# Expert gate and up weights in slabs of four rows of one matrix, and column groups of 256 columns

## The chip, the core and the metric

The kernel runs on one core of a Trainium2 chip. The metric is the device time of one execution in microseconds (us). A core has TensorE (PE; its weight loads are listed as PEld), VectorE (DVE), ScalarE (ACT), GpSimd (POOL) and SyncE (SP), which here issues the large loads. Everything is in float32; the profile shows a float32 product as two matmuls and two weight loads, and counts in it are of these.

## The reference

The input is 256 latent tokens and 256 context tokens of width 1024. Two layers of a first block (attention, Fourier mixing, and a mixture of experts) are followed by two layers of a second block with linear projections and attention. The change lies in the mixture of experts:

```
def expert_choice_ffn(h, w_router, w_gate_e, w_up_e, w_down_e):
    B, N, _ = h.shape
    cap = CAPACITY_FACTOR * N // N_EXPERTS
    aff = jax.nn.softmax((h @ w_router).astype(jnp.float32), axis=-1)
    top_aff, top_idx = lax.top_k(aff.transpose(0, 2, 1), cap)
    bidx = jnp.arange(B)[:, None, None]
    xg = h[bidx, top_idx]
    a = jnp.einsum("becd,edf->becf", xg, w_gate_e)
    u = jnp.einsum("becd,edf->becf", xg, w_up_e)
    out = jnp.einsum("becf,efd->becd", jax.nn.silu(a) * u, w_down_e) * top_aff[..., None].astype(h.dtype)
    return jnp.zeros_like(h).at[bidx, top_idx].add(out)
```

There are 16 experts, each takes 32 tokens of a token set, and gate, up and down are 1024 x 1024 each: 12 MiB of weights an expert and layer. Layer 0 has two token sets (latent and context), layer 1 one.

## The kernel before

**The ring.** All large weights pass through `ring`, four slots of 2 MiB, in the order of `slab_plan` (L52). SyncE (L597 to L603) waits until the slot's old slab is released (`slab_used`, counted by TensorE's `last_release`, L715), and issues the DMAs of the next slab as `loads` (L302) lists them. TensorE waits for a slab in `slab_wait`.

**An expert** has six slabs. Slabs 0 to 3 each hold 256 rows of the gate matrix and the same 256 rows of the up matrix, two rows for each partition (two DMAs of 1 MiB, 8 KB in a row for each partition). Slabs 4 and 5 hold 512 rows each of the down matrix, four rows for each partition (one DMA of 2 MiB, 16 KB in a row). The plan weaves in some slabs of the memory projection (xkv) in experts 6 to 13 of layer 1. A few slabs of expert 1 are loaded ahead of time by GpSimd into free buffers (`EARLY`, `load_early`, L617).

**The gate and up product** (L1142 to L1166) works with four column groups of TensorE, 32 columns wide each: the gathered tokens of an expert (`XGT`, 128 x 32) are the stationary operand, and the weights in the ring are the moving operand. Groups 0 and 1 take 512 columns each of gate, groups 2 and 3 of up, and each writes all 512 columns of its own 32 partitions of bank `ps[s]`, one bank for each token set `s`. A slab gives two row steps `k`, so 16 recorded matmuls of 512 columns for a token set.

**Behind it** ACT copies the bank into `GU` (L1760). TensorE turns it with four transposes (L1181), whose stationary operand is `GU` at every fourth column, so that channel 4p + c comes to partition p, as the down matrix has its rows. ACT makes the sigmoid of the gate part (L1771), DVE multiplies it by gate (L2378) and by up (L2383) into `HE`. The down product (L1194) is made by four column groups of 256 columns each. DVE scales and places its rows (L2395). From the fifth expert on each expert also scatters rows of an earlier group of four (L1125), and in the first twelve the rows for the next group of four are gathered (L1024, then ACT at L1705).

**Rows by pairs.** Since a slab has rows 2p and 2p + 1 in partition p, the 1024 channels of the tokens are dealt out in the same manner, by `paired` (L289): in the transposes of the normed tokens (L981), in the gathers (L1024), in the columns of the ada product for the second norm (L697), in the router table and in three vectors (`PAIRED`, L248, turned at L679 and copied at L2053).

Of the kernel before, what the change touches and what calls it, by code (L numbers as in the profile page):

```python
# [19 lines left out]
ALU = mybir.AluOpType  # L20
# [3 lines left out]
P = 128  # L24
D = 1024
# [138 lines left out]
def build(nc, a, out, ctx):  # L164
# [136 lines left out]

    def loads(kind, l, s):  # L302
# [310 lines left out]
    def _(gp):  # L613
        def load(dst, src, name):
            gp.dma_start(dst, src).then_inc(sem(name), 16)

        def load_early(l, q):  # L617

            for half, name in zip(EARLY_AT[l, q], ("w_gate_e", "w_up_e")):
                load(half.rearrange("p (k n) -> p k n", k=2),  # L620
                     a[name][l, 1, 2 * P * q:2 * P * (q + 1), :].rearrange("(p k) n -> p k n", p=P), f"early{l}{q}")
# [10 lines left out]
        for l in range(DEPTH):  # L632
# [8 lines left out]
            load(WR[:, l].rearrange("p (q i) e -> p q i e", i=2), a["w_router"][l].rearrange("(q p i) e -> p q i e", p=P, i=2), "ld_const")  # L641
# [29 lines left out]
    def _(pe):  # L671
# [285 lines left out]
        def experts(l):  # L957
# [1814 lines left out]
```

## Time and profile before

| what | value |
|---|---|
| runs, median (lowest to highest) | 2285.1 us (2284.4 to 2285.84), 3 runs |
| the profiled execution | 2280.98 us, its span 2279.1 us |
| TensorE busy, share of the span | 1986.8 us, 87% |
| VectorE, ScalarE busy | 623.2 us, 435.3 us |
| bytes moved by DMA, mean rate | 576.03 MB, 253 GB/s |
| granted TensorE clock, mean | 0.969 |

The profile is of one execution. Its span is the time from the first to the last instruction in it; the execution's own time has a little more around it. A busy time is the union of an engine's instructions. "Idle before" is the time in which an engine stood still ahead of an instruction, with the one that released it behind the arrow. A granted clock of 1.00 is 2.4 GHz, and one of 0.50 would be 1.2 GHz; values between are means over a stretch.

### The profile page before, as it was taken

To read this page: it belongs to the slowest core of one execution; us is meant where nothing else is said; L and a number is where in the kernel's file an instruction comes from. 1 tells how busy PE (TensorE), PEld (TensorE's weight loads), DVE (VectorE), ACT (ScalarE), POOL (GpSimd) and SP (SyncE) were. 2 spreads that over 40 slices of the span, in tenths; PEclk is the share of its full clock that TensorE was granted. 3 is DMA by queue.
4 is the path that set the end of the run, shared out by engine and by line. 5 is a ranking of instruction groups with operands and counts; after the bars stand their busy time and mean duration, and the time that the engine had idled before them with its cause. 6 is when DMAs were issued, how large, how long until landed. Compare 5 with 4: busy or idle time off the path is not lost.

```text
span 2279.1 us, 31723 instructions
## 1 busy us (share of the span) xinstructions
PE 1986.8 (87%) x13681; PEld 1093.5 (48%) x13681; DVE 623.2 (27%) x1483; ACT 435.3 (19%) x1095; POOL 26.9 (1%) x52
## 2 busy tenths in 40 slices
PE   7999999999988898889999975667776699999997
PEld 4445554456434444334768641233432347564765
DVE  2012640135112221223351321201101235333533
ACT  2122621013111111002161110100000122222222
POOL 3000000000000000000000000000000000000000
PEclk9999999999999999999999997889989999999999
DMA  9544244227899999994314589999999933233320
GB/s 290 185 160 173 75 142 171 94 74 272 349 424 421 423 422 422 420 419 170 129 57 185 217 353 424 423 416 415 418 415 419 364 111 111 87 135 111 111 83 19
DMA packets 133832, 576.03 MB, mean 253 GB/s; under 512 B 7448, under 2 KB 16128, under 8 KB 92736
## 3 DMA queue, kind: packets, MB, share of 16 engines
q1 hardware_dynamic: 129312, 556.82, 61.8%
q0 software_dynamic: 3872, 17.00, 2.2%
q8 instruction: 110, 1.80, 0.3%
q10 hardware_dynamic: 512, 0.19, 0.0%
q14 instruction: 26, 0.21, 0.0%
HBM read 572.93 MB, written 1.05 MB: 252 GB/s over the span
## 4 chain that ended last, share of the span: by engine, by line
PE 53%; DMA 19%; issue 10%; PEld 8%; DVE 5%; PEldq 2%; ACT 2%; SPq 0%; POOL 0%; DVEq 0%; POOLq 0%
DMA ring<-w_up_e 14%; PE ps L788 8%; PE ps L1159 6%; PE ps L1250 5%; PE ps L973 4%; PE ps L1258 3%; PEld ps L1194 3%; PE ps L804 2%; PE ps L1392 2%; PE ps L777 2%; PEldq L717 2%; DMA ring<-w_xkv 2%; DMA ring<-w_down_e 2%; PE ps L1226 1%; PE ps L1229 1%
## 5 line engine op out<-in xcount | busy, mean ns | idle before, releaser
L1159 PE MATMUL ps<-ring,reg_bc 128*32 128x512 f32 x2960 | 382.4, 653 | 125.9 <-DMA ring<-w_up_e 118.1
L1159 PEld LDWEIGHTS ps<-ring,reg_bc 128*32 128x32 f32 x2960 | 91.9, 115 | 393.7 <-DMA ring<-w_up_e 199.8
L788 PE MATMUL ps<-reg_a,ring 128*128 128x512 f32 (+1 forms) x768 | 253.9, 488 | 5.5 <-issue 4.4
L788 PEld LDWEIGHTS ps<-reg_a,ring 128*128 128x128 f32 x768 | 143.5, 190 | 104.6 <-issue 92.7
L2352 DVE TENSOR_TENSOR xall<-xall,ps 128x512 f32<-128x512 f32 x48 | 32.8, 687 | 446.0 <-PE ps L1125 446.0
L1250 PE MATMUL ps<-ring,reg_a 128*128 128x512 f32 (+2 forms) x448 | 142.7, 474 | 2.6 <-issue 2.3
L1760 ACT ACTIVATE reg_bc<-ps 128x512 f32<-128x512 f32 x48 | 28.7, 597 | 562.4 <-PE ps L1159 562.4
L2395 DVE TENSOR_TENSOR reg_a<-ps,reg_e 32x256 f32<-32x256 f32 x192 | 80.7, 420 | 199.8 <-PE ps L1194 197.4
L1194 PE MATMUL ps<-ring,reg_bc 128*32 128x256 f32 x2048 | 117.8, 380 | 16.2 <-issue 14.7
L777 PE MATMUL ps<-ring,reg_a 128*128 128x512 f32 (+1 forms) x288 | 112.8, 546 | 1.9 <-issue 1.5
L1250 PEld LDWEIGHTS ps<-ring,reg_a 128*128 128x128 f32 x448 | 74.0, 190 | 65.1 <-issue 63.7
L1194 PEld LDWEIGHTS ps<-ring,reg_bc 128*32 128x32 f32 x2048 | 70.3, 110 | 54.7 <-issue 21.1
L1194 PE MATMUL ps<-ring,reg_e 128*32 128x256 f32 x1024 | 67.2, 406 | 31.4 <-issue 17.6
L1258 PE MATMUL ps<-reg_a,ring 128*128 128x256 f32 x384 | 88.9, 390 | 6.1 <-ACT reg_d L1798 5.0
L804 PE MATMUL ps<-reg_d,ring 128*128 128x512 f32 (+1 forms) x256 | 84.2, 488 | 1.7 <-issue 0.8
L973 PE MATMUL ps<-ring,reg_bc 128*128 128x512 f32 x192 | 84.2, 594 | 0.6 <-issue 0.5
L1258 PEld LDWEIGHTS ps<-reg_a,ring 128*128 128x128 f32 x384 | 74.0, 196 | 17.0 <-issue 7.0
L777 PEld LDWEIGHTS ps<-ring,reg_a 128*128 128x128 f32 x288 | 54.2, 190 | 56.2 <-issue 54.5
L804 PEld LDWEIGHTS ps<-reg_d,ring 128*128 128x128 f32 x256 | 48.1, 190 | 35.6 <-issue 30.4
L1568 ACT ACTIVATE reg_e<-ps 128x512 f32<-128x512 f32 (+1 forms) x48 | 23.6, 491 | 207.9 <-PE ps L788 207.8
L1194 PEld LDWEIGHTS ps<-ring,reg_e 128*32 128x32 f32 x1024 | 34.5, 116 | 57.1 <-issue 29.2
L1705 ACT ACTIVATE reg_bc<-ps,modt,scl 128x128 f32<-128x128 f32 x96 | 36.2, 458 | 129.2 <-PE ps L1024 129.2
(356 smaller groups left out, 2161.5 us busy)
## 6 DMA issues: line engine op xcount, KB each, us to landing
ring<-w_down_e SPq DMA_DIRECT2D x64, 2048.0 KB, 14.9
ring<-w_gate_e SPq DMA_DIRECT2D x123, 1024.0 KB, 10.6
ring<-w_up_e SPq DMA_DIRECT2D x123, 1024.0 KB, 13.6
ring<-w_in SPq DMA_DIRECT2D x34, 2048.0 KB, 8.1
ring<-w_ada SPq DMA_DIRECT2D x24, 2048.0 KB, 8.2
ring<-w_out SPq DMA_DIRECT2D x8, 2048.0 KB, 7.9
ring<-w_xkv SPq DMA_DIRECT2D x8, 1024.0 KB, 14.1
ring<-w_br_global SPq DMA_DIRECT2D x4, 1024.0 KB, 6.4
```

The source lines that it names most:

```text
L717: pe.drain().then_inc(slab_used, 1)
L777: mm = pe.matmul(ps[t][:, c0:COL], HT[:, k, t * P:t * P + P], w[:, k, c0:COL], start=(k == 0), stop=(k == KC - 1))
L788: mm = pe.matmul(ps[j][:, 0:n], w[:, k, j * P:(j + 1) * P], HT[:, k, 0:n], start=(k == 0), stop=(k == KC - 1))
L804: mm = pe.matmul(ps[n % 4][:, 0:tokens], w[:, k, j * P:(j + 1) * P], OT[:, k, 0:tokens], start=(k == k0), stop=(k == k1 - 1))
L973: mm = pe.matmul(ps[b][:, :], MT[:, k, t * P:t * P + P], w[:, k, :], start=(k == 0), stop=(k == KC - 1))
L1159: mm = pe.matmul(ps[s][32 * j:32 * j + 32, :], XGT[l][:, e // 4, s, 2 * q + k, e % 4 * CAP:(e % 4 + 1) * CAP], w[j // 2][:, k, (j % 2) * C ...
L1194: mm = pe.matmul(ps[4 + s][32 * j:32 * j + 32, 0:SEQ], HE[l][:, s, k, q * CAP:(q + 1) * CAP], w[:, k, j * SEQ:(j + 1) * SEQ], start=(q == ...
L1250: fill(name, lambda b: [pe.matmul(ps[b][:, 0:c1 - c0], src[:, k, t * P:t * P + P], w[:, k, c0:c1], start=(k == 0), stop=(k == KC - 1)) for ...
L1258: fill(name, lambda b: [pe.matmul(ps[b][:, 0:SEQ], w[:, k, c * P:(c + 1) * P], src[:, k, :], start=(k == 0), stop=(k == KC - 1)) for k in ...
L1392: yield pe.matmul(ps[b][:, :], OT2[:, k, t * P:t * P + P], w[:, k, :], start=(q == 0), stop=(q == KC - 1))
L1705: ins = act.activation(XGT[l][:, g, s, k, :], ps[6 + h][:, kk * P:(kk + 1) * P], ACT.Identity, scale=SCL[:, l, 1, k, s:s + 1], bias=MODT[: ...
L2395: ins = dve.tensor_tensor(OE[l][r:r + CAP, e // 4 % 2, s, j * SEQ:(j + 1) * SEQ], ps[4 + s][CAP * j:CAP * (j + 1), 0:SEQ], GB[CAP * j:CAP ...
```

## The change

**Slabs.** Slab 0 and 1 of an expert now hold 512 rows of gate each, slab 2 and 3 the same of up, four rows for each partition, by one DMA of 2 MiB. The early slabs keep two DMAs of 1 MiB, each with two of the four rows.

**Column groups.** Each of the four groups takes 256 columns of the one matrix. Group j takes those of the half j // 2 whose number modulo 4 is 2 (j mod 2) or one more, so the moving operand is read at a stride of four floats, and the output stands in one piece of 256 columns, gate in the left half of the bank and up in the right. A slab gives four row steps, so 32 recorded matmuls of 256 columns for a token set.

**Behind it.** The transposes read adjacent columns of `GU`. Their outputs, the sigmoid and the two products are pieces of 256 columns, and the down product picks its stationary columns from `HE` accordingly.

**Rows by fours.** `paired` and what follows it go by four rows instead of two. The wait for the second half of the gathered rows stands ahead of slab 1 instead of slab 2.

```diff
@@ GU, EG, RG, HE, PAIRED
-        EG.append(reg_bc[:, eg:eg + ns * SEQ].rearrange("p (s c n) -> p s c n", s=ns, c=4))
+        EG.append(reg_bc[:, eg:eg + ns * SEQ].rearrange("p (s n) -> p s n", s=ns))
...
-    PAIRED = reg_e[0:24, 0:2 * P]
+    PAIRED = reg_e[0:12, 0:4 * P]
@@ paired, loads
-        return slice(k // 2 * 2 * P + k % 2, (k // 2 + 1) * 2 * P, 2)
+        return slice(k // 4 * 4 * P + k % 4, (k // 4 + 1) * 4 * P, 4)
...
+    def gate_or_up(l, e, part):
+
+        rows4 = a[("w_gate_e", "w_up_e")[part // 2]][l, e, 4 * P * (part % 2):4 * P * (part % 2 + 1), :]
+        return rows4.rearrange("(p k) n -> p k n", p=P)
...
-                return [(c0, 2, D, a[name][l, e, 2 * P * part:2 * P * (part + 1), :].rearrange("(p k) n -> p k n", p=P))
-                        for c0, name in ((0, "w_gate_e"), (2 * D, "w_up_e"))]
+                return [(0, 4, D, gate_or_up(l, e, part))]
@@ load_early
-            for half, name in zip(EARLY_AT[l, q], ("w_gate_e", "w_up_e")):
-                load(half.rearrange("p (k n) -> p k n", k=2),
-                     a[name][l, 1, 2 * P * q:2 * P * (q + 1), :].rearrange("(p k) n -> p k n", p=P), f"early{l}{q}")
+            for n, half in enumerate(EARLY_AT[l, q]):
+                load(half.rearrange("p (k n) -> p k n", k=2), gate_or_up(l, 1, q)[:, 2 * n:2 * n + 2, :], f"early{l}{q}")
@@ turn_biases
-            for i in range(2):
-                pe.transpose(ps[0][:, P + 24 * i:P + 24 * (i + 1)], PAIRED[:, i:2 * P:2], ident[0:24, 0:24])
+            for i in range(4):
+                pe.transpose(ps[0][:, P + 12 * i:P + 12 * (i + 1)], PAIRED[:, i:4 * P:4], ident[0:12, 0:12])
@@ the experts on TensorE
-                    w = [half.rearrange("p (k n) -> p k n", k=2) for half in gate_up]
-                    if q % 2 == 0 and e % 4 == 0:
-                        pe.wait_ge(*at(f"xgt@{l}", (e // 4 + 1) * 2 * ns - 1 + q // 2))
+                        pairs2 = slot(i)[:, 0:2 * D], slot(i)[:, 2 * D:4 * D]
+                    w = [two.rearrange("p (k q i r) -> p k q r i", k=2, q=2, r=4) for two in pairs2]
+                    up, half = q // 2, q % 2
+                    if q < 2 and e % 4 == 0:
+                        pe.wait_ge(*at(f"xgt@{l}", (e // 4 + 1) * 2 * ns - 1 + q))
...
-                        for k in range(2):
+                        for k in range(4):
                             for j in range(4):
-                                mm = pe.matmul(ps[s][32 * j:32 * j + 32, :],
-                                               XGT[l][:, e // 4, s, 2 * q + k, e % 4 * CAP:(e % 4 + 1) * CAP],
-                                               w[j // 2][:, k, (j % 2) * COL:(j % 2 + 1) * COL],
-                                               start=(q == 0 and k == 0), stop=(q == 3 and k == 1))
+                                mm = pe.matmul(ps[s][32 * j:32 * j + 32, up * SEQ:(up + 1) * SEQ
+                                                     ].rearrange("p (r i) -> p r i", r=2),
+                                               XGT[l][:, e // 4, s, 4 * half + k, e % 4 * CAP:(e % 4 + 1) * CAP],
+                                               w[k // 2][:, k % 2, j // 2, 2 * (j % 2):2 * (j % 2) + 2, :],
+                                               start=(half == 0 and k == 0), stop=(half == 1 and k == 3))
...
-                        mm = pe.transpose(ps[2 + s][:, c * P:(c + 1) * P], GU[l][:, s, c:COL:4], ident[:, :])
+                        mm = pe.transpose(ps[2 + s][:, c * P:(c + 1) * P], GU[l][:, s, c * P:(c + 1) * P], ident[:, :])
...
-                                               HE[l][:, s, k, q * CAP:(q + 1) * CAP],
+                                               HE[l][:, s, k % 2 * P + (2 * q + k // 2) * CAP:k % 2 * P + (2 * q + k // 2 + 1) * CAP],
@@ the sigmoid on ACT, the products on DVE
-                    gate = ps[2 + s][:, :].rearrange("p (c n) -> p c n", c=4)[:, :, 0:2 * CAP]
-                    act.activation(EG[l][:, s], gate, ACT.Sigmoid).then_inc(sem(f"eg@{l}"), 1)
+                    act.activation(EG[l][:, s], ps[2 + s][:, 0:SEQ], ACT.Sigmoid).then_inc(sem(f"eg@{l}"), 1)
...
-                    dve.tensor_tensor(HE[l][:, s], RG[l][:, s], turned[:, :, 2 * CAP:4 * CAP], ALU.mult
+                    dve.tensor_tensor(HE[l][:, s], RG[l][:, s], ps[2 + s][:, SEQ:COL], ALU.mult
```

The lines below are the order of instructions on one engine. `ps` is PSUM, `ring` the weight ring, `reg_bc` holds `XGT`, `GU` and `HE` of layer 0, `tmp` the selection matrices and `reg_d` the normed tokens; here the counts are of products as the engine gets them in the program, grouped, with one row for a run of equal instructions. TensorE, one middle expert of layer 0 and the start of the next, before:

```order
L1159 MATMUL ps<-ring,reg_bc 32x512 x64
L1125 MATMUL ps<-reg_a,reg_e 128x512 x2
L1181 MATMUL ps<-ident,reg_bc 128x128 x8
L1194 MATMUL ps<-ring,reg_bc 32x256 x32
L1024 MATMUL ps<-tmp,reg_d 128x128 x8
L1194 MATMUL ps<-ring,reg_bc 32x256 x32
L1035 MATMUL ps<-ident,reg_e 128x128 x2
```

And the same place now:

```order
L1163 MATMUL ps<-ring,reg_bc 32x256 x128
L1128 MATMUL ps<-reg_a,reg_e 128x512 x2
L1186 MATMUL ps<-ident,reg_bc 128x128 x8
L1199 MATMUL ps<-ring,reg_bc 32x256 x32
L1027 MATMUL ps<-tmp,reg_d 128x128 x8
L1199 MATMUL ps<-ring,reg_bc 32x256 x32
L1038 MATMUL ps<-ident,reg_e 128x128 x2
```

The 64 gate and up products of 512 columns have become 128 of 256; nothing else has moved. SyncE, the head of the expert slabs of layer 0 behind the last ada slabs, before:

```order
L602 DMA ring<-w_out 128x8x512 x2
L602 DMA ring<-w_ada 128x8x512 x4
L602 DMA ring<-w_gate_e 128x2048
L602 DMA ring<-w_up_e 128x2048
...
L602 DMA ring<-w_down_e 128x4096 x2
```

And now:

```order
L606 DMA ring<-w_out 128x8x512 x2
L606 DMA ring<-w_ada 128x8x512 x4
L606 DMA ring<-w_gate_e 128x4096 x2
L606 DMA ring<-w_up_e 128x4096 x2
L606 DMA ring<-w_down_e 128x4096 x2
```

Four pairs of gate and up DMAs have become two DMAs of gate and two of up, each of the shape of the down slabs.

## Rows read from the trace of the kernel before

**Rows 1.** The page: the chain that ended last by line, and a DMA issue.
```profile
DMA ring<-w_up_e 14%; PE ps L788 8%; PE ps L1159 6%; PE ps L1250 5%; PE ps L973 4%; PE ps L1258 3%; PEld ps L1194 3%; PE ps L804 2%; PE ps L1392 2%; PE ps L777 2%; PEldq L717 2%; DMA ring<-w_xkv 2%; DMA ring<-w_down_e 2%; PE ps L1226 1%; PE ps L1229 1%
...
ring<-w_gate_e SPq DMA_DIRECT2D x123, 1024.0 KB, 10.6
```

**Rows 2.** Groups by line: count, busy us, mean ns, idle before and releasers.
```profile
L1159 PE MATMUL ps<-ring,reg_bc 128*32 128x512 f32 x2960 | 382.4, 653 | 125.9 <-DMA ring<-w_up_e 118.1 <-issue 4.8
```

**Rows 3.** Windows: us, busy PE, PEld, DVE, ACT, POOL; granted clock, DMA share, GB/s.
```profile
700.00:760.00 60.00, 53.05 (x560) 23.83 (x556) 13.04 (x30) 6.31 (x16) 0.00 (x0) 1.00 1.01 423
1520.00:1580.00 60.00, 41.67 (x289) 22.03 (x282) 5.15 (x12) 3.88 (x9) 0.00 (x0) 0.91 1.02 416
```

**Rows 4.** Timeline of TensorE, layer 0: start us, us, operation, idle before and releaser.
```profile
556.13 7.38 PE L1159 MATMUL ps<-ring,reg_bc 128*32 128x512 f32 x64 [0.30 <-issue]
...
671.12 7.39 PE L1159 MATMUL ps<-ring,reg_bc 128*32 128x512 f32 x64
...
702.44 11.13 PE L1159 MATMUL ps<-ring,reg_bc 128*32 128x512 f32 x96 [0.29 <-issue]
...
714.27 3.64 PE L1159 MATMUL ps<-ring,reg_bc 128*32 128x512 f32 x32 [0.70 <-DMA ring<-w_up_e]
...
720.14 1.12 PE L1181 MATMUL ps<-ident,reg_bc 128*128 128x128 f32 x8
...
722.21 3.66 PE L1194 MATMUL ps<-ring,reg_bc 128*32 128x256 f32 x64 [0.95 <-issue]
...
732.23 7.38 PE L1159 MATMUL ps<-ring,reg_bc 128*32 128x512 f32 x64 [0.29 <-issue]
...
913.52 7.39 PE L1159 MATMUL ps<-ring,reg_bc 128*32 128x512 f32 x64
...
940.76 3.64 PE L1159 MATMUL ps<-ring,reg_bc 128*32 128x512 f32 x32 [0.27 <-issue]
...
1023.22 7.42 PE L1194 MATMUL ps<-ring,reg_bc 128*32 128x256 f32 x128 [0.94 <-issue]
```

**Rows 5.** Timeline, layer 1: the first slab, then the slabs of one expert.
```profile
1325.86 3.96 PE L1159 MATMUL ps<-ring,reg_bc 128*32 128x512 f32 x32
1325.97 1.51 ACT L1705 ACTIVATE reg_bc<-ps,modt,scl 128x128 f32<-128x128 f32 x4 [0.38 <-PE ps L1024]
...
1386.14 1.93 PE L1194 MATMUL ps<-ring,reg_e 128*32 128x256 f32 x32 [1.46 <-DMA ring<-w_down_e]
...
1391.10 3.62 PE L1159 MATMUL ps<-ring,reg_bc 128*32 128x512 f32 x16 [3.03 <-DMA ring<-w_up_e]
...
1396.09 1.93 PE L1159 MATMUL ps<-ring,reg_bc 128*32 128x512 f32 x16 [1.37 <-DMA ring<-w_up_e]
...
1406.05 1.92 PE L1159 MATMUL ps<-ring,reg_bc 128*32 128x512 f32 x16 [1.64 <-DMA ring<-w_up_e]
...
1415.84 3.22 PE L1194 MATMUL ps<-ring,reg_e 128*32 128x256 f32 x32 [1.91 <-DMA ring<-w_down_e]
```

**Rows 6.** Instructions of single lines: duration ns min/median/max, first and last start.
```profile
L1181 PEld LDWEIGHTS ps<-ident,reg_bc x192: 195/209/221, 577.1 to 1792.4; 128*128 128x128 f32 x192
...
L981 PEld LDWEIGHTS ps<-ident,reg_d x48: 194/209/231, 495.8 to 1303.3; 128*128 128x128 f32 x48
...
L743 PEld LDWEIGHTS ps<-ident,reg_d x32: 139/140/143, 1038.0 to 1058.5; 128*128 128x128 f32 x32
...
L697 PE MATMUL ps<-ring,ct x1536: 272/273/422, 13.5 to 1311.3; 128*32 128x128 f32 x192
...
L1159 PE MATMUL ps<-ring,reg_bc x2960: 589/592/1063, 556.1 to 1790.4; 128*32 128x512 f32 x198
```

**Rows 7.** Timeline of TensorE: ada products at stride two, adjacent, and adjacent transposes.
```profile
190.99 2.04 PE L697 MATMUL ps<-ring,ct 128*32 128x128 f32 x64
...
208.67 1.95 PE L697 MATMUL ps<-ring,ct 128*32 128x128 f32 x64
...
1050.12 1.04 PE L743 MATMUL ps<-ident,reg_d 128*128 128x128 f32 x8
```

More of the change, by code:

```diff
@@ L242, in build @@
         GU.append(reg_bc[:, gu:gu + ns * COL].rearrange("p (s n) -> p s n", s=ns))
-        EG.append(reg_bc[:, eg:eg + ns * SEQ].rearrange("p (s c n) -> p s c n", s=ns, c=4))
-        RG.append(reg_bc[:, rg:rg + ns * SEQ].rearrange("p (s c n) -> p s c n", s=ns, c=4))
+        EG.append(reg_bc[:, eg:eg + ns * SEQ].rearrange("p (s n) -> p s n", s=ns))
+        RG.append(reg_bc[:, rg:rg + ns * SEQ].rearrange("p (s n) -> p s n", s=ns))
         hidden = reg_e[:, 1024:1280] if he is None else reg_bc[:, he:he + ns * SEQ]
-        HE.append(hidden.rearrange("p (s c n) -> p s c n", s=ns, c=4))
+        HE.append(hidden.rearrange("p (s n) -> p s n", s=ns))
         OE.append(reg_a[:, 0:2048 * ns].rearrange("p (b s d) -> p b s d", b=2, s=ns))
-    PAIRED = reg_e[0:24, 0:2 * P]
+    PAIRED = reg_e[0:12, 0:4 * P]
     YT = reg_e[:, 4096:5120].rearrange("p (b n) -> p b n", b=2)
@@ L640, in _ @@
                      a[f"diff_lambda_{v}_2"][l:l + 1, :].broadcast_to([P, 32]), "ld_const")
-            load(WR[:, l].rearrange("p (q i) e -> p q i e", i=2), a["w_router"][l].rearrange("(q p i) e -> p q i e", p=P, i=2), "ld_const")
+            load(WR[:, l].rearrange("p (q i) e -> p q i e", i=4), a["w_router"][l].rearrange("(q p i) e -> p q i e", p=P, i=4), "ld_const")
         for t in range(2):
@@ L1145, in experts @@
                         pe.wait_ge(sem(f"early{l}{q}"), 32)
-                        gate_up = EARLY_AT[l, q]
+                        pairs2 = EARLY_AT[l, q]
                     else:
@@ L1942, in _ @@
             for n, v in enumerate((a["b_ada"][l, 3 * D:4 * D], a["b_ada"][l, 4 * D:5 * D], a["norm2_g"][l])):
-                load_vec("ld_vec0", PAIRED[12 * l + 4 * n:12 * l + 4 * n + 4, :], v.rearrange("(q c) -> q c", c=2 * P))
+                load_vec("ld_vec0", PAIRED[6 * l + 2 * n:6 * l + 2 * n + 2, :], v.rearrange("(q c) -> q c", c=4 * P))
         act.wait_ge(*at("vec1t", 1))
@@ L2049, in bias_columns @@
             link(dve.tensor_copy(vec0t[:, :], ps[0][:, 0:P]))
-            pairs_in = ps[0][:, P:P + 48].rearrange("p (i l n q) -> p l n q i", i=2, l=DEPTH, n=3)
+            pairs_in = ps[0][:, P:P + 48].rearrange("p (i l n q) -> p l n q i", i=4, l=DEPTH, n=3)
             for l in range(DEPTH):
                 for n, c in enumerate((24, 32, 56)):
-                    ins = dve.tensor_copy(vec0t[:, 64 * l + c:64 * l + c + 8].rearrange("p (q i) -> p q i", i=2),
+                    ins = dve.tensor_copy(vec0t[:, 64 * l + c:64 * l + c + 8].rearrange("p (q i) -> p q i", i=4),
                                           pairs_in[:, l, n])
@@ L2375, in experts @@
                     m = e * ns + s
-                    turned = ps[2 + s][:, :].rearrange("p (c n) -> p c n", c=4)
                     dve.wait_ge(*at(f"eg@{l}", m + 1))
-                    dve.tensor_tensor(RG[l][:, s], EG[l][:, s], turned[:, :, 0:2 * CAP], ALU.mult
+                    dve.tensor_tensor(RG[l][:, s], EG[l][:, s], ps[2 + s][:, 0:SEQ], ALU.mult
                                       ).then_inc(sem(f"rg@{l}"), 1)
```

1 line of the change is left out of this document (removed).

## Prediction

> **What bounds the kernel now.** I read the chain and the DMA issues on the page, the groups by line, the windows over the two expert stretches, and last TensorE's timeline inside one expert of each layer. The chain that ended last has the DMA of w_up_e as its first single item, 14% [rows 1]. The gate and up product, L1159, is the costliest group: 2960 recorded matmuls, 382 us busy, 118 us of idle time ended by that DMA [rows 2]. The change touches almost nothing outside the expert stretches (556 to 1031 us in layer 0, from 1326 us on in layer 1), so I took one window in each. In both the DMA engines are full, share 1.01 and 1.02, at 423 and 416 GB/s; in layer 0 TensorE is busy 53 us of 60 beside that, in layer 1 only 42 [rows 3]. So both are bound by transfers, layer 1 with room to spare, layer 0 with TensorE close behind.
>
> How close shows in the timeline of layer 0 [rows 4]. One expert starts its gate product at 702.44 us, the next at 732.23: 29.79 us, of which TensorE waited 0.70 for a DMA. Its own work is 29.1 us. From 671.12 to 913.52 experts 4 to 11 pass, 30.3 us each. The other eight gather no rows or scatter none and have less to do: expert 12 takes 27.24 us (913.52 to 940.76).
>
> **What the transfers gain.** In layer 1 TensorE waits for each slab, so its starts are the landings [rows 5]. Gate/up slabs land 4.96 us after what went before (1386.14 to 1391.10), 4.99, and the next two 9.96 together; the two down slabs behind them take 9.79 together, 4.90 each. All are 2 MiB. A gate/up slab is now two DMAs with 8 KB runs for each partition, a down slab one DMA with 16 KB runs; after the change every expert slab has exactly the second form. That is 0.07 us a slab. There are 123 gate/up slabs [rows 1]; some four at the head of each layer have landed before they are wanted, which leaves 115: 115 x 0.07 = 8 us, four in each layer. The transfers of one expert then take 6 x 4.90 = 29.4 us instead of 29.7. Whether the longer runs or the DMA fewer give it, I can't tell, and both go together. The bound below is nothing: if a down slab is quick only for what goes before it, there is no gain.
>
> The Trainium skill, "DMA: Bandwidth & Descriptors" (Anatomy of one DMA), gives each DMA a fixed 2 us beside its bytes over 436 GB/s; by that, 123 DMAs fewer would save up to 246 us. The landings speak against it: pairs of 1 MiB land every 4.98 us, so the fixed part already lies beside other transfers.
>
> **What TensorE pays.** Three edits meet on it.
>
> First, the gate/up matmuls are twice as many and half as wide. The down product has that form already: 64 matmuls of 256 columns take 3.66 us, 32 of 512 take 3.64 [rows 4]. The twice as many weight loads lie under the streaming there as well. 0.02 us a slab of layer 0, 0.1 us an expert.
>
> Second, the transposes of the hidden rows read adjacent columns and no longer every fourth. Their weight loads take 209 ns in the median, loads of adjacent columns 140 [rows 6]; eight such transposes took 1.12 us [rows 4], eight of adjacent columns 1.04 [rows 7]. That gives back 0.1 us an expert, on the path from the gate to the down product. The two cancel. Sigmoid and products read the same elements of PSUM, now in one piece: 0, between a few tens of ns either way.
>
> Third, and this decides: each matmul now reads its moving operand, the weights in the ring, at a stride of four floats. No row shows that form. The nearest is the ada product, four column groups of 128 columns: 64 matmuls take 1.95 us where columns are adjacent and 2.04 where they are every second one [rows 7], 0.09 more. If that is a price of the instruction, a slab of layer 0, now 64 matmuls, pays 0.09, an expert 0.36. If it is a pace of reading, more comes out: 2.04 less the 0.27 of one matmul [rows 6], over 15 steps of four, is 118 ns for 128 columns; the wide product takes 3.64 less 0.59 over 7 steps, 436 ns for 512 columns, 109 for 128. Nine ns for each 128 columns, 32 such a slab: 0.3 us, 1.2 an expert. The bounds are nothing, should the wide streams hide it, and twice the streaming time. Of stride four against stride two only weight loads tell: the transposes at four (L1181) and at two (L981) both load in 209 ns [rows 6]. A longer stride cost nothing there, so I stay with the nearest row, 0.36.
>
> Own work of a middle expert becomes 29.1 + 0.1 - 0.1 + 0.36 = 29.5 us, against 29.4 of transfers: level. I let layer 0 keep half of its 4 us, since the two now trade waits. Layer 1 keeps all: with one set of tokens a slab costs TensorE 1.9 us, and 3.6 at the low clock, inside 4.9 [rows 5].
>
> **Small edits.** The router table, the norm vectors, the ada columns and the turned tiles go by four instead of two. Two transposes more at the start, 0.3 us each, lie beside the first weight DMA; the gathers' weight loads go from stride two to four, no change by the two medians above. The second half of the gathered rows is wanted at slab 1 instead of slab 2: in layer 1 ACT finishes it at 1325.97 + 1.51 = 1327.48 us, and the first slab's products, begun at 1325.86 and 1.9 long, end at 1327.8 [rows 5]. So 0, and a few tenths of a us once if that cover goes. SyncE issues one DMA where it issued two; it waits for free slots, not for issue: 0. The slabs that POOL loads early stay two DMAs of 1 MiB: 0.
>
> **Sum.** -4 in layer 1, -2 in layer 0: -6 us on the profiled execution of 2281.0 us, 2275. The median of the runs lies 4.1 us higher, so I forecast 2279.
>
> **Rivals.**
> *The stride is a pace.* 1.2 us an expert: own work 30.3, above 29.4. The middle eight then take what they take now, 30.3; the first four, which find slabs landed, pay 5 us; layer 1 gives 4; some waits for DMAs stay. +4, between 0 and +12: about 2289. For it: the 118 ns. Against it: 0.09 us can as well be a gap in a row of 64 short instructions.
>
> *Every column opens a new line of SBUF (slower).* At stride four each float lies 16 bytes on, and four column groups read at once. At half pace a slab of layer 0 goes from 3.64 to 7.3 us, an expert's own work from 29.1 to 43.7. The middle eight: 8 x (43.7 - 30.3) = 107. The other eight, which now take 232 us of the 474.5 between 556.13 and the end of the last down product (1023.22 + 7.42), 29.0 each: 8 x (27.2 + 14.6 - 29.0) = 102. Less layer 1's 4: +205, 2490. It decides from some 0.3 us a slab on; at a fifth more streaming time, 0.7 us, it is 8 x 1.6 + 8 x 1.0 - 4 = +17, 2302. Against it: 209 ns at stride two and at four alike. For it: no moving operand is read so here, and never by four groups at once.
> The Trainium skill, "SBUF — State Buffer" (Door 1: The DMA port swizzle), states such a rule: lines of 16 bytes, at least two hits on a line for full speed. The weight-load rows don't agree: they pay at stride two, where two hits remain, and no more at four.
>
> *The transfers gain nothing.* Then layer 0 pays up to 2 us, layer 1 nothing: 2285 to 2287.
>
> **Chances.** Forecast 0.48, pace 0.24, new lines 0.17, no gain 0.11. A measurement of this kernel tells a change from none from about 0.2% on, 4.6 us. The forecast's own range is -11 to -3, mostly beyond that: faster 0.44. Same, 2280.5 to 2289.7: the rest of the forecast, the case without gain, half of the pace: 0.25. Slower, the other half and the new lines: 0.31. The range goes from 2274, where all of the 8 us and the shorter transposes are kept, to 2303, a fifth more streaming time, which takes in the pace; it leaves out the strong form of new lines and a little more.
>
> **What would show it.** Gate/up slabs of layer 1 landing 4.90 us apart and not 4.98: the gain is there. The 64 strided matmuls of a slab of layer 0 in 3.66 to 3.75 us: forecast; near 4.0: pace; 4.3 and more: new lines, with a DMA share in the windows of layer 0 below 1.0 and under 400 GB/s. The transposes of L1181 at 140 ns a load. The forecast is wrong if layer 0's stretch grows beyond 474.5 us, or if layer 1 doesn't shrink by at least 3.

## The result, and the profile after

| | before | after |
|---|---|---|
| median (lowest to highest) | 2284.75 us (2282.17 to 2285.84), 4 runs | 2568.66 us (2565.67 to 2570.11), 4 runs |
| ratio, with its 95% interval | | 1.1243 (1.1223 to 1.1262) |
| span of the profiled execution | 2279.1 us | 2563.7 us |
| TensorE busy | 1986.8 us, 87% | 2362.9 us, 92% |
| VectorE, ScalarE busy | 623.2, 435.3 us | 623.2, 435.4 us |
| granted TensorE clock, mean | 0.969 | 0.991 |

The change costs 284 us. The forecast was 2279 with 2303 as its upper end: it is wrong, and in its sign too. The rival of the new lines, 2490, is the one that has its side.

The page of the kernel after, the chain that ended last by engine and by line, the costliest groups (busy us, mean ns, idle before and its releaser), and the DMA issues:

```profile
PE 73%; DMA 8%; issue 8%; PEld 4%; DVE 4%; ACT 2%; PEldq 1%; SPq 0%; DVEq 0%
...
L1163 PE MATMUL ps<-ring,reg_bc 128*32 128x256 f32 x5920 | 695.0, 632 | 43.3 <-DMA ring<-w_up_e 18.8
...
L1027 PEld LDWEIGHTS ps<-tmp,reg_d 128*128 128x128 f32 x384 | 91.3, 328 | 15.6 <-issue 14.9
...
L1199 PE MATMUL ps<-ring,reg_bc 128*32 128x256 f32 x2048 | 117.1, 380 | 16.3 <-issue 14.8
...
ring<-w_up_e SPq DMA_DIRECT2D x63, 2048.0 KB, 9.8
ring<-w_gate_e SPq DMA_DIRECT2D x60, 2048.0 KB, 8.9
```

The gate and up product, L1163 now, is busy for 695.0 us where it was 382.4, and its idle time falls from 125.9 to 43.3 [rows 2]: in layer 0, as the rows below show, TensorE no longer waits for weights, the weights wait for TensorE. One of its matmuls takes 632 ns. The down product L1199 has the same form, 32 stationary columns and 256 moving ones from the same ring, and takes 380. What differs is that it reads adjacent columns.

The windows after, two in layer 0 and three in layer 1 (columns as in [rows 3]), and below them the first 60 us of layer 1 before:

```profile
720.00:780.00 60.00, 57.39 (x542) 22.89 (x538) 5.38 (x14) 3.85 (x9) 0.00 (x0) 1.00 0.75 277
840.00:900.00 60.00, 56.80 (x574) 27.70 (x578) 10.76 (x26) 5.36 (x13) 0.00 (x0) 1.00 0.73 268
...
1597.00:1657.00 60.00, 53.98 (x471) 24.73 (x474) 5.04 (x12) 6.48 (x16) 0.00 (x0) 0.97 0.77 306
1657.00:1717.00 60.00, 43.96 (x434) 14.93 (x430) 11.78 (x45) 9.21 (x16) 0.00 (x0) 0.97 1.00 421
...
1980.00:2040.00 60.00, 52.00 (x436) 25.44 (x432) 6.41 (x14) 3.50 (x8) 0.00 (x0) 1.00 1.01 424
```

```profile
1326.00:1386.00 60.00, 43.57 (x396) 17.53 (x391) 5.87 (x14) 7.43 (x18) 0.00 (x0) 0.89 0.96 400
```

In layer 0 the DMA engines have fallen from 1.01 and 423 GB/s [rows 3] to 0.75 and 277, TensorE is busy 57 of 60 us at full clock: the bound has changed. In layer 1 they are full again from the second window on, but the first moves 306 GB/s where it moved 400.

TensorE's timeline after, the head and layer 0, then layer 1 (columns as in [rows 4]):

```profile
559.23 3.92 PE L700 MATMUL ps<-ring,ct 128*32 128x128 f32 x64
...
564.40 7.73 PE L1027 MATMUL ps<-tmp,reg_d 128*128 128x128 f32 x32 [0.51 <-DVE tmp L2273]
...
576.24 7.50 PE L1163 MATMUL ps<-ring,reg_bc 128*32 128x256 f32 x64 [0.29 <-issue]
...
805.75 30.15 PE L1163 MATMUL ps<-ring,reg_bc 128*32 128x256 f32 x256 [0.29 <-issue]
...
837.98 1.04 PE L1186 MATMUL ps<-ident,reg_bc 128*128 128x128 f32 x8
...
844.06 3.97 PE L1027 MATMUL ps<-tmp,reg_d 128*128 128x128 f32 x16 [0.39 <-issue]
...
851.91 30.07 PE L1163 MATMUL ps<-ring,reg_bc 128*32 128x256 f32 x256 [0.29 <-issue]
...
1291.79 7.42 PE L1199 MATMUL ps<-ring,reg_bc 128*32 128x256 f32 x128 [0.99 <-issue]
...
1597.51 3.81 PE L1163 MATMUL ps<-ring,reg_bc 128*32 128x256 f32 x32
...
1675.97 3.81 PE L1163 MATMUL ps<-ring,reg_bc 128*32 128x256 f32 x32 [1.84 <-DMA ring<-w_gate_e]
1680.86 3.82 PE L1163 MATMUL ps<-ring,reg_bc 128*32 128x256 f32 x32 [1.08 <-DMA ring<-w_gate_e]
1685.75 3.88 PE L1163 MATMUL ps<-ring,reg_bc 128*32 128x256 f32 x32 [1.07 <-DMA ring<-w_up_e]
...
2083.26 1.93 PE L1199 MATMUL ps<-ring,reg_e 128*32 128x256 f32 x32 [0.80 <-DMA ring<-w_down_e]
```

A slab of layer 0 takes 7.50 us and not 3.64. An expert has no wait for a DMA left; the next begins 46.16 us behind it (805.75 to 851.91) where it was 30.3 [rows 4]. The 284.6 us between the two spans stand in four places:

| stretch | before | after | more |
|---|---|---|---|
| up to the first slab of layer 0 | 556.13 | 576.24 | 20.1 |
| layer 0, to the end of its last down product | 474.5 | 723.0 | 248.5 |
| from there to the first slab of layer 1 | 295.2 | 298.3 | 3.1 |
| layer 1, to the end of its last down product | 475.0 | 487.7 | 12.7 |

**Layer 0.** 64 slabs at 7.50 - 3.64 = 3.86 us more are 247. Twelve gathers of 16 matmuls take 3.97 us each; the row of one before, from its timeline in layer 0:

```profile
696.44 2.12 PE L1024 MATMUL ps<-tmp,reg_d 128*128 128x128 f32 x16 [0.36 <-issue]
```

12 x 1.85 = 22. The transposes L1186 give 16 x 0.1 back. That is 267; the stretch has grown by 248.5, so some 19 us of what is added don't show. TensorE's idle time in the stretch falls from 51.5 to 37.6 us, which is 14 of them: work now lies where TensorE waited before. The last 5 stay open.

**Layer 1.** Slabs land 4.89 us apart (1675.97, 1680.86, 1685.75), as the forecast has it, and the stretch is longer all the same. A slab costs TensorE 3.81 us and no longer 1.92, so it hands slots back later at the head, where slabs lie ready: in the first 60 us (400 - 306) GB/s x 60 us = 5.6 MB fewer arrive, which is 13.3 us of transfers at 424 GB/s. That is the whole 12.7. Behind those 60 us the mean rate to the end of the stretch is 418 GB/s in both kernels, so the faster landings bring nothing there: one window of 60 us (1897 to 1957) has only 401 GB/s, with TensorE busy for 54.8 us of it. The granted clock of the stretch is 0.88 before, where TensorE is busy 324 of 475 us, and 0.99 after, where it is busy 413 of 488.

**The head.** Eight ada products for the second norm read every fourth column now, 3.84 to 3.92 us each and not 2.04 [rows 7], and four gathers stand ahead of the first slab: 12 x 1.85 = 22, of which 20 show.

### The profile page after: what moved, and what is told of

Read it like the earlier page. It is cut to its first block, busy times and chain, and to the rows that moved or that the text cites. A ratio compares the mean times of both kernels' runs of the same rounds, so it can differ in the third digit from the quotient of the medians.

```text
span 2563.7 us, 37748 instructions
## 1 busy us (share of the span) xinstructions
PE 2362.9 (92%) x16755; PEld 1257.1 (49%) x16755; DVE 623.2 (24%) x1483; ACT 435.4 (17%) x1095; POOL 26.8 (1%) x52
## 4 chain that ended last, share of the span: by engine, by line
PE 73%; DMA 8%; issue 8%; PEld 4%; DVE 4%; ACT 2%; PEldq 1%; SPq 0%; DVEq 0%
PE ps L1163 23%; PE ps L791 8%; PE ps L1199 5%; PE ps L1255 4%; DMA ring<-w_up_e 4%; PE ps L1027 3%; PE ps L976 3%; PE ps L1263 3%; PE ps L807 2%; PE ps L1397 2%; PE ps L780 2%; PE ps L700 2%; PE ps L1128 2%; DMA ring<-w_down_e 1%; PE ps L502 1%
## 5 line engine op out<-in xcount | busy, mean ns | idle before, releaser
L1163 PE MATMUL ps<-ring,reg_bc 128*32 128x256 f32 x5920 | 695.0, 632 | 43.3 <-DMA ring<-w_up_e 18.8
L1163 PEld LDWEIGHTS ps<-ring,reg_bc 128*32 128x32 f32 x5920 | 210.4, 125 | 509.8 <-issue 450.3
L1199 PE MATMUL ps<-ring,reg_bc 128*32 128x256 f32 x2048 | 117.1, 380 | 16.3 <-issue 14.8
L1027 PE MATMUL ps<-tmp,reg_d 128*128 128x128 f32 x384 | 94.6, 404 | 6.6 <-issue 5.9
L1027 PEld LDWEIGHTS ps<-tmp,reg_d 128*128 128x128 f32 x384 | 91.3, 328 | 15.6 <-issue 14.9
L1199 PEld LDWEIGHTS ps<-ring,reg_bc 128*32 128x32 f32 x2048 | 70.1, 110 | 55.2 <-issue 21.6
L1199 PE MATMUL ps<-ring,reg_e 128*32 128x256 f32 x1024 | 63.4, 388 | 26.9 <-issue 21.9
L700 PE MATMUL ps<-ring,ct 128*32 128x128 f32 x1536 | 65.6, 331 | 3.7 <-DMA ring<-w_ada 3.7
```

The lines of the kernel that those rows point to most:

```text
L700: mm = pe.matmul(ps[b][32 * j:32 * j + 32, 0:P], CT[:, k, :], w[:, k, paired(j) if 6 <= s < 10 else slice(j * P, j * P + P)], start=(k == ...
L1027: mm = pe.matmul(ps[6 + h][:, kk * P:(kk + 1) * P], XN[:, 2 * s + t, paired(k)], SEL[:, s, t, g * P:(g + 1) * P], start=(t == 0), stop=(t ...
L1163: mm = pe.matmul(ps[s][32 * j:32 * j + 32, up * SEQ:(up + 1) * SEQ].rearrange("p (r i) -> p r i", r=2), XGT[l][:, e // 4, s, 4 * half + k, ...
L1199: mm = pe.matmul(ps[4 + s][32 * j:32 * j + 32, 0:SEQ], HE[l][:, s, k % 2 * P + (2 * q + k // 2) * CAP:k % 2 * P + (2 * q + k // 2 + 1) * CAP],
```

## The experiments

What is measured in each is the row of its first slab in layer 0: 64 matmuls of 256 columns, four column groups at once, so 16 steps of four. Kernels with one run have no interval. They differ from the kernel before by 1.8% and more, but e2 lies only 0.4% above e1 and e3 0.15% above the kernel after; what is read from these is the slab, not the time.

**One group of runs: only the stride of the moving operand.** The four kernels are the kernel after with another view of the same slab, and as many columns. The output of each matmul is one piece of 256 adjacent columns of the bank in all of them, so the writing side stays as it is.

```diff
-  w[k // 2][:, k % 2, j // 2, 2 * (j % 2):2 * (j % 2) + 2, :]   # after: every 4th column
+  w[k // 2][:, k % 2, j * SEQ:(j + 1) * SEQ]                    # e1: adjacent
+  w[k // 2][:, k % 2, j // 2, j % 2, :]                         # e2: every 2nd
+  w[k // 2][:, k % 2, 64 * j:64 * j + 768:3]                    # e5: every 3rd
+  w[k // 2][:, k % 2, 2 * j:2 * j + 2, :]                       # e3: every 8th
```

> The changed kernel, but each column group of the gate and up product reads 256 adjacent columns of the weights instead of every fourth (so the channels come out in another order, and the output differs); all else, the four-row slabs, the 256-column matmuls, the gathers and ada columns at stride four, stays. Theory (lines of 16 bytes: what costs is that each column opens a new one): the 64 matmuls of a slab of layer 0 go from 7.4-7.5 us to 3.66; what stays is 20 us ahead of layer 0, 3 ahead of layer 1, 1.9 us for each gather, less the faster landings: 2300 to 2320. Rival (the form costs: twice as many matmuls, four groups writing two places of a bank): the slab stays above 6 us and the time above 2500.

> As e1_adjacent, but every second column (8 bytes apart; output differs). If a line costs 1.77 ns and a column 0.83 ns, whichever is more, two columns on a line come to 0.885 ns a column: 16 steps of 256 columns 0.227 us apart, the slab of layer 0 about 3.9 us, the time 10 to 25 us over e1_adjacent. If only the second hit on a line matters, as the rule of two hits says, there is no difference to e1_adjacent. If any stride halves the pace: 7.4 us a slab.

> As e1_adjacent, but every third column (12 bytes apart; groups overlap, output differs). Three of four columns open a new line: 1.33 ns a column, steps 0.34 us apart, slab 5.6 us, time 2400 to 2430. If it is all or nothing at 16 bytes: 3.7 to 3.9 us a slab. If every column that has no second hit pays in full: near 5.6 as well.

> As the changed kernel, but every eighth column (32 bytes apart; output differs). A line of 16 bytes: no more than at stride four, slab 7.4 to 7.5 us, time within 10 us of the changed kernel's 2569. If the four groups contend for banks, or if lines are of 32 bytes, it is clearly slower than stride four, up to 15 us a slab.

The rows of the timeline, e1, e2, e5 and e3 in turn:

```profile
576.05 3.66 PE L1163 MATMUL ps<-ring,reg_bc 128*32 128x256 f32 x64 [0.29 <-issue]
```

```profile
579.54 3.83 PE L1163 MATMUL ps<-ring,reg_bc 128*32 128x256 f32 x64 [0.28 <-issue]
```

```profile
576.05 5.69 PE L1163 MATMUL ps<-ring,reg_bc 128*32 128x256 f32 x64 [0.29 <-issue]
```

```profile
574.32 7.57 PE L1163 MATMUL ps<-ring,reg_bc 128*32 128x256 f32 x64 [0.29 <-issue]
```

| columns | time of the kernel | slab | one matmul | step | lines of 16 bytes a step | ns a line |
|---|---|---|---|---|---|---|
| adjacent (e1) | 2314.92 us, 4 runs | 3.66 us | 379 ns | 0.219 us | 256 | 0.85 |
| every 2nd (e2) | 2323.66, 1 run | 3.83 | 388 | 0.229 | 512 | 0.448 |
| every 3rd (e5) | 2441.95, 1 run | 5.69 | 510 | 0.345 | 768 | 0.450 |
| every 4th (after) | 2568.66, 4 runs | 7.50 | 632 | 0.458 | 1024 | 0.447 |
| every 8th (e3) | 2572.47, 1 run | 7.57 | 640 | 0.462 | 1024 | 0.451 |

A step is the slab less one matmul (its median), over 15; its 1024 columns open so many lines of 16 bytes as the table says. From stride two on the step is 0.447 to 0.451 ns for each line, within 1%, and from stride four to eight it doesn't grow: what is paid is the line, not the distance. Adjacent columns are bound by something else, 0.219 us for 1024 columns, 0.214 ns each. The step is the longer of the two, 0.214 ns a column or 0.448 ns a line. The cut is not an all or nothing at stride four: stride three pays already, and two per line pay 0.17 us a slab. The times came out as expected but for two: e5 lies 12 us above its 2400 to 2430, and e2 only 9 us over e1, where 10 to 25 were expected.

The ada products of the kernel after give the same price from another instruction, four groups of 128 columns at stride four:

```profile
140.57 3.84 PE L700 MATMUL ps<-ring,ct 128*32 128x128 f32 x64
```

One of its matmuls takes 0.41 us in the median, so a step is (3.84 - 0.41) / 15 = 0.229 us for 512 columns on 512 lines: 0.447 ns a line.

e1 is also the proof of place: with the stride gone, and that alone, 254 of the 284 us go. What is left, a ratio of 1.0135 (1.0113 to 1.0157), the next experiments divide.

**Adjacent pairs (e4), and rows dealt by DVE (e6).** e4 deals out the columns otherwise: group j takes two adjacent columns of every four. The output stands in one piece as before the edit, and the transposes read `GU` by twos. e6 also has DVE write the normed rows in the order by fours, so that the turned tiles and the gathers read adjacent columns.

```diff
+  two.rearrange("p (k q i h r) -> p k q h i r", k=2, q=2, h=2, r=2)      # e4, e6: pairs 16 bytes apart
+  GU[l][:, s, c // 2 * SEQ + c % 2:(c // 2 + 1) * SEQ:2]
+  XN[:, t, :].rearrange("p (q r i) -> p q i r", q=2, r=4)                # e6: what DVE writes
+  XN[:, 2 * s + t, k * P:(k + 1) * P]                                    # e6: what a gather reads
```

> The changed kernel, the same 256 columns for each group, but read in pairs: two adjacent columns, then the next two 16 bytes on; the transposes behind it pick every second column of the bank. Two columns to a line of 16 bytes, so 0.895 ns a column: slab of layer 0 3.83 us as in e2_stride2, time 2320 to 2330. If it is the step to the next place that costs, not the lines per column: above 5.5 us a slab. If adjacent pairs cost nothing: 3.66 and 2315.

> e4_pairs, and DVE writes the normed rows dealt out by fours, so that gathers and turned tiles load adjacent columns. Theory (stationary loads at stride four pay by the line too, 330 ns instead of 190): 16 matmuls of a gather take 1.9 us instead of 3.9, the stretch before layer 0 is 8 us shorter, and an expert's own work falls by 1.9 us in the first twelve: 20 to 30 us under e4_pairs, 2293 to 2305. The ada columns at stride four still cost 15 us. DVE's strided write of 1024 columns may take longer than 0.81 us; six of them.

e4: 2325.58 us (2 runs), ratio 1.0182 (1.0147 to 1.0216), slab 3.87 us: pairs read as every second column does, since they open as many lines. e6: 2295.91 us (4 runs), 1.0053 (1.0034 to 1.0073), 30 us less than e4 on the same chip; e4's two runs lie 7 us apart, so the 30 are uncertain by some us. The lines of single instructions in the kernel after (duration in ns, lowest/median/highest):

```profile
L1027 PEld LDWEIGHTS ps<-tmp,reg_d x384: 307/330/337, 551.5 to 1899.9; 128*128 128x128 f32 x192
...
L984 PEld LDWEIGHTS ps<-ident,reg_d x48: 195/212/260, 503.8 to 1572.8; 128*128 128x128 f32 x48
...
L1186 PEld LDWEIGHTS ps<-ident,reg_bc x192: 138/140/145, 612.5 to 2078.7; 128*128 128x128 f32 x192
```

The gather's load in the kernel before, by twos:

```profile
L1024 PEld LDWEIGHTS ps<-tmp,reg_d x384: 192/196/337, 539.4 to 1612.1; 128*128 128x128 f32 x192
```

The lines of e6, and what DVE pays:

```profile
L1027 PEld LDWEIGHTS ps<-tmp,reg_d x384: 186/192/332, 551.1 to 1625.8; 128*128 128x128 f32 x192
...
L984 PEld LDWEIGHTS ps<-ident,reg_d x48: 138/140/223, 502.2 to 1319.3; 128*128 128x128 f32 x48
...
L2210 DVE TENSOR_SCALAR reg_d<-xall,st x6: 1283/1307/1362, 492.8 to 1317.2; 128x1024 f32<-128x1024 f32 x6
```

A gather's weight load of every fourth column takes 330 ns, of adjacent ones 192, and before, by twos, it took 196 in the median. The load of a transpose goes from 212 to 140 only. A transpose's load pays at stride two and no more at four [rows 6]; a plain load pays nothing at two and 1.7 times at four. The one could not speak for the other. The dealing costs DVE 0.5 us for each of six instructions, 1307 against 814 ns in the kernel after.

**The rest of the head (f3).** e6 with the ada columns adjacent.

```diff
-  w[:, k, paired(j) if 6 <= s < 10 else slice(j * P, j * P + P)]
+  w[:, k, j * P:j * P + P]
```

> e6_pairs_dealt with the ada products of the second norm reading adjacent columns again (their channels then come in another order, and the output differs). Eight products of 64 matmuls at 1.95 us instead of 3.9: 15 us less than e6's 2296, so 2278 to 2284, which would close the account: what is left over before is 0.2 us a slab for the pairs against 8 us of faster landings. Rival: some of the ada products lie beside other waits, then 2285 to 2290.

2285.94 us (10 runs), 1.0005 (0.9995 to 1.0014): 10 us off e6, and level with the kernel before. Every ada product takes 1.95 us, and layer 0 begins at 557.20 us, where it was 568.42 in e6. The theory had 15 us; the rival named beside it, 2285 to 2290, is what came. The four ada products of layer 0's own norm give their full 1.9 us each; of the 7.7 us of the other four, just ahead of the experts, some 4.6 show in the profiles. With it the loss is accounted for: 254 us for the stride of the moving operand (after to e1); 30 for gathers and turned tiles (e4 to e6) and 10 for the ada columns (e6 to f3), less the 7 that the transfers gain (d1, below). The last three make 33, where e1 still loses 31 by its ratio and 33 by its medians; with e4's scatter that is agreement to a few us, no closer. Pairs cost up to 64 x 0.2 = 13 us in layer 0 (e4 is 11 us above e1), which eats up what the transfers gain.

**Which part of the DMA gains (d1, d2, d3).** The kernel before with other slabs, and nothing else: one DMA of 16 KB runs, as after; one DMA of 8 KB runs; two DMAs of one matrix.

```diff
+  return [(0, 4, D, rows4.rearrange("(p k) n -> p k n", p=P))]                  # d1: 16 KB in a row
+  return [(0, 2, 2 * D, rows4.rearrange("(b p r) n -> p b (r n)", p=P, b=2))]   # d2: 8 KB in a row
+  return [(2 * D * h, 2, D, rows4[2 * P * h:2 * P * (h + 1), :].rearrange("(p k) n -> p k n", p=P))
+          for h in range(2)]                                                    # d3: two DMAs
```

> The kernel before with one thing of the change: a gate/up slab is one DMA of 512 rows of one matrix, four rows in a row for each partition; the products go on as before, so they multiply other weights and the output differs. Theory (the transfers gain 0.07 to 0.09 us a slab, whoever computes): gate/up slabs of layer 1 land 4.90 us apart, time 6 to 9 us under before. Rival (down slabs only look quick): 4.98 and no change.

> As d1_one_dma_16k, one DMA for each slab, but in runs of 8 KB for each partition (two blocks of 256 rows, two rows each). If the number of DMAs gives the gain: landings 4.90 us apart, and d1's time. If the length of the runs gives it: 4.98 and the time of before.

> As d2_one_dma_8k, the same bytes in the same runs of 8 KB to the same places, but two DMAs a slab, both of one matrix. Like before in all but the matrix that a DMA reads: 4.98 us between landings and no change of time under the rule that number or length of runs count. If two matrices read side by side cost, it comes out faster than before.

d1: 2277.41 us (5 runs), 0.9965 (0.9952 to 0.9979). d2: 2285.24 us (11), 1.0004 (0.9995 to 1.0014). d3: 2284.29 us (11), 0.9998 (0.9989 to 1.0007). Slabs of one expert in layer 1, of d1:

```profile
1393.26 1.93 PE L1159 MATMUL ps<-ring,reg_bc 128*32 128x512 f32 x16 [2.88 <-DMA ring<-w_gate_e]
1398.15 3.47 PE L1159 MATMUL ps<-ring,reg_bc 128*32 128x512 f32 x16 [2.97 <-DMA ring<-w_gate_e]
1403.05 1.92 PE L1159 MATMUL ps<-ring,reg_bc 128*32 128x512 f32 x16 [1.43 <-DMA ring<-w_up_e]
1407.93 3.01 PE L1159 MATMUL ps<-ring,reg_bc 128*32 128x512 f32 x16 [2.96 <-DMA ring<-w_up_e]
```

and of d2:

```profile
1393.39 1.92 PE L1159 MATMUL ps<-ring,reg_bc 128*32 128x512 f32 x16 [1.15 <-DMA ring<-w_gate_e]
1398.36 3.51 PE L1159 MATMUL ps<-ring,reg_bc 128*32 128x512 f32 x16 [3.05 <-DMA ring<-w_gate_e]
1403.34 1.92 PE L1159 MATMUL ps<-ring,reg_bc 128*32 128x512 f32 x16 [1.46 <-DMA ring<-w_up_e]
1408.29 3.55 PE L1159 MATMUL ps<-ring,reg_bc 128*32 128x512 f32 x16 [3.03 <-DMA ring<-w_up_e]
```

4.89 us a slab against 4.97. The gain is that of the longer runs; a DMA fewer gives nothing. In d1's profile the stretch of layer 0 is 472.2 us (559.28 to 1031.5) and that of layer 1 471.2 (1328.22 to 1799.43), 2.3 and 3.8 less than before: the forecast's 2 and 4. These are one profile each, and whole runs of one kernel scatter by a few us, so the two halves are less certain than their sum.

**Pairs with rows by twos (g).** e6 with one DMA of 8 KB runs for a slab, and rows, router table and vectors by twos as before, dealt by DVE.

```diff
-  return slice(k // 4 * 4 * P + k % 4, (k // 4 + 1) * 4 * P, 4)
+  return slice(k // 2 * 2 * P + k % 2, (k // 2 + 1) * 2 * P, 2)
```

> Slabs of one matrix by one DMA, but in two blocks of 256 rows with two rows for each partition; row tables and ada columns by twos as before; 256 columns to a group read in pairs; normed rows dealt out by twos. Nothing reads at stride four any more. Own work of a middle expert 29.1 + 0.7 (pairs) - 0.2 (gathers and transposes): about 29.7 against 29.4 to 29.8 of transfers. Theory: 2275 to 2290; under 2280 only if one DMA a slab is what makes landings faster.

2291.86 us (10 runs), 1.0024 (1.0012 to 1.0037), with slabs of 3.83 to 3.88 us: 2 us above the range expected. It is 4 us better than e6, about what the ada columns by twos give back (10 us in f3) less the 7 us of the long runs that it gives up, and still slower than before, with no transfer gained and 0.2 us a slab paid. Of the kernels here that compute what the reference does (the kernel after, e4, e6, g, e7, f2), none is faster than the kernel before; d1 gains its 7 us with the wrong weights multiplied.

**Where the limit sits (e7, f1, f2).** e7 and f2 are the kernel after with its matmuls in another order: one group after the other, or groups 0 and 1, then 2 and 3. f1 is e1 with one group after the other.

```diff
-  for k in range(4):
-      for j in range(4):
+  for j in range(4):                                              # e7, f1
+      for k in range(4):
+  for k, j in [(k, j) for two in range(2) for k in range(4) for j in (2 * two, 2 * two + 1)]:   # f2
```

> The changed kernel with the loops over column groups and row steps exchanged, so that the matmuls of one group follow each other and the four groups' streams hardly overlap. If the pace of one line in 1.79 ns is each stream's own, 64 matmuls of a slab of layer 0 take 64 x 0.458 = 29 us, and the time is 4500 us or more. If the four streams hold each other up, each alone reads at 0.83 ns a column: 64 x 0.213 = 13.7 us, the time 3000 to 3300.

> The control to e7_groups_in_turn: the groups one after the other, but reading adjacent columns (output differs). e7 took 16.4 us for the 64 matmuls of a slab, 0.250 each. If one stream alone reads at stride four as fast as adjacent columns, this one takes 16.4 us as well and the time is near 3443. If stride four costs one stream something, this one is down to 13.7 us (64 x 0.213) and under 3200.

> The changed kernel, stride four, but groups 0 and 1 run their four row steps together, then groups 2 and 3: half the streams at a time, twice the steps. If what is short is one port that serves all streams with a line of 16 bytes each 0.447 ns, two streams need 2 x 0.447 = 0.894 ns a column: 32 steps of 0.229 us, 7.4 us a slab, 8.6 if the weight loads show as in e7; time 2565 to 2650, although nothing is gained or lost in lines. If the pace belonged to a stream (1.79 ns a column), the slab would take 32 x 0.458 = 14.7 us.

The first slab of e7, of f1 and of f2:

```profile
578.18 16.39 PE L1163 MATMUL ps<-ring,reg_bc 128*32 128x256 f32 x64 [0.29 <-issue]
```

```profile
576.59 8.14 PE L1163 MATMUL ps<-ring,reg_bc 128*32 128x256 f32 x64 [0.29 <-issue]
...
L1163 PEld LDWEIGHTS ps<-ring,reg_bc x5920: 106/110/178, 576.6 to 2143.6; 128*32 128x32 f32 x198
```

```profile
576.00 9.26 PE L1163 MATMUL ps<-ring,reg_bc 128*32 128x256 f32 x64 [0.29 <-issue]
```

The kernels take 3443.42, 2630.55 and 2755.00 us, one run each. e7 refutes the 29 us of the first theory, and lies above the 13.7 of the second. For f1, stride four does cost a group alone something, and the time is under 3200, but the 13.7 us missed: it took over the pace that a group has while four run. f2 is nearer to the shared limit than to a pace of each stream, and above both of its figures, 8.6 us and 2650. Worked out as above: a group alone needs (8.14 - 0.38) / 63 = 0.123 us for 256 adjacent columns, 0.48 ns each, and (16.39 - 0.63) / 63 = 0.250 us at stride four, 0.98 ns for each line. Two groups at once need (9.26 - 0.63) / 31 = 0.278 us a step of two, 1.09 ns for each column of a group; four at once need 0.458, 1.79 ns. So there are two limits. A group alone took 0.98 ns for a line of its own at stride four, twice its 0.48 ns for an adjacent column. The 0.48 need not be a pace of reading: f1's weight loads take 0.110 us each in the median, close to its 0.123, and may set it; e7's take 0.128, half of its 0.250. All groups together took no less than 0.45 ns a line, and it is this one that binds four groups: on its own limit, each would do its 256 columns in 0.250 us and not in 0.458. Had the shared limit been the only one, e7 would take about 7.5 us and not 16.39. What remains open is f2's 0.278 us where the two limits give 0.250, whether the weight loads have a part in it, and from which stride a group alone pays; that was not tried.

## Why the prediction was wrong

- **"The third, and this decides", 0.36 us an expert: wrong, and it is the error.** It measured 4 x 3.86 = 15.4 us. The step that failed is this term of the sum: the price of stride four was carried over from the ada product at stride two, 0.09 us a slab, where the slab pays 3.86. What let it pass is the choice of the nearest row for the step from two to four. The proxy was a transpose's weight load, 209 ns at stride four and at two, and from it I concluded that a longer stride costs nothing. A transpose's load is another kind of reading than the stream of a moving operand by four groups, and not even like a gather's load (330 against 192 ns). The argument "against" new lines rested on the same row and falls with it.
- **The right row was in the text.** The ada product at stride two against adjacent [rows 7] is a moving operand read by four groups, and the prediction works out its step: 118 ns against 109. Taken per line it says 118 ns for 256 lines, 0.46 ns a line, just above what the columns cost; at stride four the lines double and the step with them: 0.236 us for 512 columns, 0.47 for 1024, against the 0.458 measured. (The lines of 16 bytes were in the rival's text.) I had read it only per column, as "nine ns for each 128 columns", where small means harmless. It was small since two limits happen to be level at stride two.
- **The rival "every column opens a new line": right in mechanism.** It gave 7.3 us a slab (7.50), an expert's own work 43.7 us (46.2), 268 to 277 GB/s in layer 0 as "under 400", +205 (+284). It was short by 80: the slab's last 0.2 us, 64 of them, 13; the gathers of layer 0, 22; the head, 20; layer 1, which lost 13 and didn't gain 4; the rest, some 7, lies between the layers (3) and in its sum for layer 0 (4). I gave it 0.17. The row that decided was at hand, so it should have led.
- **The rule of the Trainium skill**, "SBUF — State Buffer" (Door 1: The DMA port swizzle), lines of 16 bytes and two hits for full speed, was set aside for the weight-load rows. The measured steps agree with the line of 16 bytes, 0.45 ns for each at strides two to eight; two hits cost 5% of a slab here (3.83 against 3.66 us), so "full" is nearly right. Its remark that one can stride over four float32 for free is not borne out: 7.50 us.
- **Small edits at 0: wrong for two of them.** "No change by the two medians" for the gathers took two medians of transposes: a gather's load takes 330 ns, 1.9 us for 16 matmuls, of which there are 24. The ada columns by four were counted at nothing, though it was the very instruction that the third term leaned on: 1.85 us each, eight of them. Together 59 us of work, and some 40 of the result (e4 to f3). DVE, the sigmoid, the early slabs and SyncE at 0: nothing in the runs speaks against it; DVE and ACT are busy to 0.1 us as before.
- **Twice as many matmuls of half the width, 0.02 us a slab: right.** e1's slab takes 3.66 us against 3.64.
- **The transposes at 140 ns, 1.04 us for eight: right**, as L1186's load and the row of 837.98 us show.
- **What the transfers gain, up to 8 us, of which the sum took 6: right**, in size (d1: 2284.34 to 2277.41, 6.9) and, as far as one profile tells, in its division, 2.3 and 3.8. The doubt left open there, runs or number of DMAs, goes to the runs. In the kernel after slabs that TensorE waits for land 4.89 us apart too, but nothing of the gain is left in the time of either layer: layer 0 no longer waits for them, and layer 1 moves 418 GB/s behind its head as before.
- **The fixed 2 us a DMA** of the Trainium skill, "DMA: Bandwidth & Descriptors" (Anatomy of one DMA), weighed at up to 246 us: d2 has 123 DMAs fewer and no gain, 1.0004 (0.9995 to 1.0014). The page has the figure for DMAs that GpSimd issues, and these are SyncE's. The landings had said so.
- **Layer 0's stretch beyond 474.5 and layer 1 not 3 shorter** were named as the signs of a wrong forecast, and both came: 723.0 and 487.7.
- **The chances** don't add up to the digit: by their own parts "same" is 0.27 and "slower" 0.29, where 0.25 and 0.31 stand. Nothing hangs on it.

## What to carry to other kernels

Before a moving operand is read at a stride, count the lines of 16 bytes that it opens for each matmul, over all column groups at work, and set that beside the columns: here, with four groups at work, the longer of 0.214 ns a column and 0.448 ns a line set the pace, and a stride of four float32 halved it. A cheap small stride is no evidence that a longer one is cheap: it may stand just where one limit meets another. A cost is safely carried over only from an instruction that reads in the same role and with as many groups. If a layout of the weights gains in the transfers (here 0.35% by runs of 16 KB), keep the columns of each group adjacent and let the price of the new order fall on the smaller operand.

## What the runs showed of the hardware that was not expected

- The step of four groups follows lines of 16 bytes within 1% from stride two to eight (0.447 to 0.451 ns a line), stride three included; the ada products at stride four give 0.447.
- A plain float32 weight load of 128 columns takes 192 ns adjacent, 196 at stride two and 330 at stride four; a transpose's load 140, 209 [rows 6] and 212.
- One column group alone, weight loads included, takes 0.123 us for each matmul of 256 adjacent columns; four at once need 0.219 us for all four. Four groups together are 2.2 times as fast as one, at stride four (4 x 0.250 against 0.458) as with adjacent columns.
- DVE writing 1024 float32 in an order by fours takes 1307 ns (e6), by twos 1228 (g), straight 814 (the kernel after).
